# A mixture-of-experts block on one core: late items get a slot order of their own, result rows begin in DRAM, and small items split their second activation part first

## What is computed

```
logits = h @ w_router + b_router
top_val, top_idx = lax.top_k(logits, 4)            # 4 of 32 experts for each token
gates = jax.nn.softmax(top_val)
hgu = lax.ragged_dot(h[tok], w_gate_up, group_sizes) + b_gate_up[e_sorted]   # [2048 rows] x [1024, 2048] per expert
act = min(glu, 7) * sigmoid(1.702 * min(glu, 7)) * (clip(lin, -7, 7) + 1)
out = (lax.ragged_dot(act, w_down, group_sizes) + b_down[e_sorted]) * gates  # x [1024, 1024] per expert
moe = segment_sum(out, tok)
h = layernorm(alpha * h + moe)
```

## Time and profile before

| | us |
|---|---|
| median of 3 runs | 1948.08 |
| lowest and highest | 1943.51, 1948.17 |
| the profiled execution | 1949.36 |
| its span, first to last instruction | 1947.7 |
| busy: PE, DVE, ACT, POOL | 1837.7, 1667.0, 1351.6, 508.4 |
| mean granted clock | 0.978 |

### The profile page before, as it was taken

The page is one execution under the profiler, slowest core; times in us unless marked ns, Lnnn a source line. Parts: engine busy times, 40 slices in busy tenths (PEclk is TensorE's granted clock), DMA queues, the critical chain, the costliest instruction groups (busy, mean ns, idle before and its releaser), DMA issues.

```text
span 1947.7 us, 28549 instructions
## 1 busy us (share of the span) xinstructions
PE 1837.7 (94%) x8415; PEld 1438.3 (74%) x8415; DVE 1667.0 (86%) x1783; ACT 1351.6 (69%) x1777; POOL 508.4 (26%) x395
## 2 busy tenths in 40 slices
PE   6999999998989998999999999999899999999887
PEld 3657767787768876877777777777777777777665
DVE  6899987348775477989999999999899999999877
ACT  4556865214346525788889888888888888898775
POOL 6671000000000105523422423423133322323121
PEclk7999999999999997999999999999899999999988
DMA  8222225332110156999999999999999999999995
GB/s 318 86 108 86 87 67 203 121 102 73 54 44 23 38 179 213 340 401 386 392 395 395 388 396 391 386 387 395 331 396 401 391 388 383 398 390 345 345 322 201
DMA packets 133073, 523.37 MB, mean 269 GB/s; under 512 B 15145, under 2 KB 20425, under 8 KB 112848
## 3 DMA queue, kind: packets, MB, share of 16 engines
q1 hardware_dynamic: 118704, 492.45, 66.5%
q0 software_dynamic: 14304, 30.11, 5.6%
HBM read 512.76 MB, written 19.29 MB: 273 GB/s over the span
## 4 chain that ended last, share of the span: by engine, by line
PE 63%; DVE 12%; DMA 10%; ACT 8%; issue 5%; SPq 1%; ACTq 0%; DVEq 0%; POOL 0%
PE ps L1150 28%; DMA arena<-in_w_gate_up 8%; PE ps L1386 5%; PE ps L1434 5%; PE ps L1199 3%; DVE split L2852 3%; PE ps L1377 3%; ACT arena_r L2047 2%; PE ps L1415 2%; PE ps L1391 2%; PE ps L1613 2%; PE ps L1482 2%; PE ps L1066 2%; ACT split L2047 2%; ACT arena L2076 1%
## 5 line engine op out<-in xcount | busy, mean ns | idle before, releaser
L1150 PE MATMUL ps<-split,xTs 128*128 128x512 f32 x2016 | 505.3, 399 | 11.3 <-DVE split L2852 7.7
L1150 PEld LDWEIGHTS ps<-split,xTs 128*128 128x128 f32 x2016 | 379.5, 191 | 106.5 <-DVE split L2852 21.0
L2852 DVE TENSOR_TENSOR split<-arena,split 128x2048 fp32r<-128x2048 f32 x166 | 377.1, 2286 | 16.6 <-ACT split L2047 14.9
L2047 ACT ACTIVATE split<-arena 128x1024 fp32r<-128x1024 f32 x332 | 330.9, 1052 | 32.0 <-DMA arena<-in_w_gate_up 25.4
L2852 DVE TENSOR_TENSOR split<-ring,split 128x2048 fp32r<-128x2048 f32 x106 | 242.8, 2305 | 0.4 <-ACT split L2047 0.4
L856 POOL DMA_INDIRECT y_rows<-arena,slots x33 | 146.2, 4431 | 345.2 <-issue 291.5
L2047 ACT ACTIVATE split<-ring 128x1024 fp32r<-128x1024 f32 x212 | 212.7, 1057 | 7.0 <-DMA ring<-in_w_gate_up 2.9
L2852 DVE TENSOR_TENSOR arena_r<-arena,arena_r 128x2048 fp32r<-128x2048 f32 x83 | 189.7, 2285 | 3.4 <-ACT arena_r L2047 3.4
L1150 PE MATMUL ps<-arena_r,xTs 128*128 128x512 f32 x672 | 182.6, 406 | 6.7 <-ACT arena_r L2047 4.9
L1150 PE MATMUL ps<-split,aTs 128*128 128x512 f32 x672 | 168.3, 396 | 15.9 <-DVE aTs L2911 15.9
L2047 ACT ACTIVATE arena_r<-arena 128x1024 fp32r<-128x1024 f32 x166 | 171.7, 1055 | 14.5 <-DMA arena<-in_w_gate_up 13.8
(11 more groups left out here) (484 smaller groups left out, 3127.0 us busy)
## 6 DMA issues: line engine op xcount, KB each, us to landing
arena<-in_w_gate_up SPq DMA_DIRECT2D x170, 1024.0 KB, 14.2
ring<-in_w_gate_up SPq DMA_DIRECT2D x102, 1024.0 KB, 14.7
arena<-in_w_down SPq DMA_DIRECT2D x79, 1024.0 KB, 14.3
ring<-in_w_down SPq DMA_DIRECT2D x57, 1024.0 KB, 14.6
ring<-in_w_in SPq DMA_DIRECT2D x23, 1024.0 KB, 5.0
ring<-in_w_out SPq DMA_DIRECT2D x8, 1024.0 KB, 5.2
ring<-in_mod_w SPq DMA_DIRECT2D x10, 512.0 KB, 9.1
ring<-in_mod_w SPq DMA_DIRECT2D x4, 1024.0 KB, 5.0
```

The source lines that it names most:

```text
L1150: m = mm(ps[:, banks + q, :], lhs[:, x_, k, :], w[:, q * 512:(q + 1) * 512], start=start, stop=stop)
L2047: A(split_part(0, c), chunk(it, c), ACT.Copy).then_inc(sig("hi_ready"), 1)
L2852: V.tensor_tensor(split_pair(1, p), slot_tile(it.slot(p)), split_pair(0, p), ALU.subtract).then_inc(sig("lo_ready"), 1)
```

## The change

There are three edits.

1. `y_dram` is begun out of `h1_dram` and not out of `h1` in SBUF, and ACT doesn't wait for `y_begun`. POOL's wait stays.
2. A late item's tiles go to the slots of `LATE_SLOTS`. For each tile `before_in` finds which tile, of the item itself or of the one before, used the slot last, and SP waits for that one. Since the one program text of the loop serves the first late item (behind a small one with the old order) and the others, the later of the two tiles is waited for. `late_item`'s counts of loads per slot follow.
3. In small items, the loop's and the late ones, ACT does `act_high(1)` ahead of `split_high(22, 23)` and DVE `act_low(1)` ahead of `split_low(10)`.

```diff
--- before.py
+++ after.py
@@ -111,17 +111,31 @@
 class Item:
 
 
-    def __init__(self, i, small, next_small, pairs, at, rows, loads, begin=0, joined=None):
+    def __init__(self, i, small, next_small, pairs, at, rows, loads, begin=0, joined=None, late=False):
         self.i, self.small, self.next_small = i, small, next_small
+        self.late = late
         self.pairs, self.at, self.rows, self.joined = pairs, at, rows, joined
         self.loads, self.begin = loads, begin
 
     def slot(self, j):
-        return (j + self.begin) % SLOTS
+        return LATE_SLOTS[j] if self.late else (j + self.begin) % SLOTS
+
+    def before_in(self, j, before):
+
+        own = [q for q in range(j) if self.slot(q) == self.slot(j)]
+        if own:
+            return self, own[-1]
+        last = before.last_in(self.slot(j))
+        if before.late:
+            last = max(last, max(q for q in range(EXPERT_TILES) if q % SLOTS == self.slot(j)))
+        return before, last
 
     def last_in(self, s):
         return max(j for j in range(EXPERT_TILES) if self.slot(j) == s)
 
+LATE_SLOTS = (6, 7, 4, 5, 0, 1, 6, 7, 4, 5, 2, 3)
+
+
 def uses(s):
     return 2 if s < EXPERT_TILES - SLOTS else 1
 
@@ -144,7 +158,7 @@
 def late_item(j, back=0):
 
     return Item(j + (BEFORE_LATE - back), True, True, j * PAIRS + (BEFORE_LATE - back) * PAIRS,
-                j + (BEFORE_LATE - back - BIG), j * 32 + ((BEFORE_LATE - back) * 32 - BIG * 16), lambda s: j * (16 * uses(s)) + 48 * (LOOPS + 1), 0, j + (BEFORE_LATE - back - BIG))
+                j + (BEFORE_LATE - back - BIG), j * 32 + ((BEFORE_LATE - back) * 32 - BIG * 16), lambda s: j * (16 * LATE_SLOTS.count(s)) + (48 * (LOOPS + 1) + 16 * (uses(s) - LATE_SLOTS.count(s))), 0, j + (BEFORE_LATE - back - BIG), True)
 
 
 
@@ -692,10 +706,7 @@
                 expert_tile(first_item(), j, 0)
             def slot_free(it, before, j):
 
-                if j < SLOTS:
-                    it, j = before, before.last_in(it.slot(j))
-                else:
-                    j = j - SLOTS
+                it, j = it.before_in(j, before)
                 wait_alone(sp, sig("lo_ready"), sp.to_reg(it.pairs + (LEAD + j + 1)))
 
             def item_tiles(it, before):
@@ -826,7 +837,7 @@
             pool.wait_ge(sig("idx0_ready"), 1)
             gather(idx_first[:, 0:1])
             for t in range(TC):
-                pool.dma_start(y_dram[t * P:(t + 1) * P, :], h1[:, t, :]).then_inc(sig("y_begun"), 16)
+                pool.dma_start(y_dram[t * P:(t + 1) * P, :], h1_dram[t * P:(t + 1) * P, :]).then_inc(sig("y_begun"), 16)
 
             pool.wait_ge(sig("oh_ready"), 1)
             by_k = lambda x: x.rearrange("p (t k) e -> p t k e", t=TC)
@@ -2051,7 +2062,6 @@
                 act.wait_ge(sig("xt_ps"), q + 1)
                 high(xTs, q, 7 - 6 * q, sig("xt_hi"), P)
             act.wait_ge(sig("h1_stored"), 16 * TC)
-            act.wait_ge(sig("y_begun"), 16 * TC)
 
             def run(it):
 
@@ -2126,8 +2136,8 @@
                     split_high(20, 22)
                     sigmoid(1)
                     next_high(0)
+                    act_high(1)
                     split_high(22, 23)
-                    act_high(1)
                     next_high(1)
                     split_high(23, 24)
                     return
@@ -2936,8 +2946,8 @@
                     act_low(0)
                     split_low(9)
                     activation(1)
+                    act_low(1)
                     split_low(10)
-                    act_low(1)
                     next_low(0)
                     split_low(11)
                     next_low(1)
```

## The result

Six runs of the changed kernel gave a median of 1929.27 us (1926.83 to 1932.83), beside 1941.41 us (1934.92 to 1948.17) for six of the kernel before. The ratio is 0.9936 with a 95% interval from 0.9915 to 0.9957: 12.4 us faster, clear of the 0.3%. The time lies in the range given, 3.3 us above the forecast. The gain is a little over half of the 22.4 us summed. That the time still came so near is in part luck: the kernel before is 6.7 us lower in the median of six runs than in that of the first three. From 1948.08 us the same ratio would have led to some 1936, still in the range but 10 us above the forecast. The profiled execution has a span of 1928.8 us (before: 1947.7), so the spans alone, at 18.9 us, would flatter the change.

What follows compares the result with a forecast made beforehand. PE, DVE and DMA were taken as nearly full in the steady stretch, with room in late items and the expert phase's start. Terms 6.8 + 17.6 - 2 = 22.4 us off 1949.4 gave 1927.0; forecast 1926, range 1917 to 1939.

Steps and rivals of the forecast that it cites:

- a gain of 17.6 us: Late items: the new slots keep loads streaming, so three items take 98.0 us on PE instead of 115.6.
- the rival of starved late items: Late items: six slots in a burst don't carry the stream; gain 9.6 instead of 17.6 us, time 1934, chance 0.12.
- The price by bytes: Late items: 12.79 MB each at the steady stretch's 388 GB/s, giving 33.0 us.
- I take 6.8, since PE is the engine without a gap after it: Expert phase start: PE's 4.9 us gap goes and 1.9 us of low clock come back.
- from about 760.5: Expert phase start: POOL can issue item 1's gather behind its store at 759.48, from about 760.5 us.
- A slower copy up to some 28 us is covered: Expert phase start: item 0's matmuls hide a DRAM to DRAM copy of up to some 28 us.
- Start hidden: Expert phase start: first items' loads or the gather set the pace, edit 1 gives nothing; 1932.5 us, chance 0.08.
- they don't absorb the gain: Expert phase start: DMA engines wait for slots, at 0.33 and 13 GB/s behind PE's gap, so the gain stays.
- sum +2 us: Small items: the new order costs 2 us in all, most of DVE's stall being absorbed by the loads.
- The full price of 18 x 0.55 = 9.9 us: Small items: upper bound of the new order's cost, 9.9 us over 18 items.
- 0.1 us each, 1.5 us: Steady stretch: full DMA engines absorb part of the stall, leaving 0.1 us in each of 15 small items, 1.5 us.
- DMA keeps the first two: Late items: DMA sets the first two, so the new order costs 0.5 us only in the last.

Runs made afterwards that it cites:

- no_order_again: The changed kernel without its third edit, run once more beside the changed kernel on one chip: 1923.48 us, ratio 0.9895 to the kernel before.
- early gather: Edits 1 and 2 without 3, with POOL issuing item 1's gather behind the third store of slot rows, not the eighth: 1924.48 us, ratio 0.9902 to before.
- only_slots: Edit 2 alone, the late items' slot order, on the kernel before: 1927.26 us against 1947.46, ratio 0.9909.
- only_order: Edit 3 alone, both engines' new order in small items, on the kernel before: 1954.93 us against 1947.46, ratio 1.0047.
- only_act_order: Only ACT's half of edit 3, on the kernel before: 1945.20 us against 1942.78, ratio 1.0008.
- only_dve_order: Only DVE's half of edit 3, on the kernel before: 1955.01 us against 1945.49, ratio 1.0065.
- no_order: The changed kernel with its third edit taken back: 1929.70 us, ratio 0.9913 to the kernel before.
- source_wait_kept: The kernel before with only the source of the result-row copies changed to DRAM, ACT's wait kept: 1940.08 us, ratio 0.9985.

## Why the prediction came out as it did

The range held and the sign was right, and so was the order of size of the largest term. Two of the three terms of the sum were mis-sized, both to the bad side.

**Edit 2, "a gain of 17.6 us": right in size and in the wait that it removes; the pace of the items behind it was met partly by luck.** Alone it measured 17.7, with an interval from 14.2 to 21.0, so the agreement to a tenth says nothing. The late items were to take 33.0, 33.0 and 32 us and took 32.7, 33.0 and 33.0 (98.7 against 98.0). The second keeps the stream full, 393 GB/s against the 388 taken, and the rival of starved late items (36 each) is out. But the stream doesn't set the 33.0: the last item takes it as well, with DMA at 0.80 and 303 GB/s, and the three kernels with edit 2 but no edit 3 and the old gather take 32.4 to 32.9, the second in `no_order_again` 32.45 at 408 GB/s. In these items DVE is the fullest engine, 31.56 of 32.97 us in the last. The price by bytes and the real pace happened to agree.

The Trainium skill's page HBM Reference, section Specifications, gives some 358 GB/s as a core's effective share, and more for a core that streams alone. The row of this case, 393 GB/s over such an item, agrees with the second and is above the first.

**Edit 1, "I take 6.8, since PE is the engine without a gap after it": the step that failed.** It measured 1.0 us alone, with an interval from a gain of 3.1 to a loss of 1.2. PE's gap and the low clock behind it did go (the window right behind the old gap, 755.88 to 760.67, has a granted clock of 1.00). But PE had a gap after it, which I priced away in the paragraph on POOL: "from about 760.5" assumed that POOL's stores keep the 0.97 us of the earlier trace rows. That row stands in a stretch where DVE is idle, as its next subtract waited 10.6 us for ACT. With the gap gone, DVE's subtracts run there, the stores beside them take up to 3.06 us each, and the gather leaves at 768.5. "A slower copy up to some 28 us is covered" looked at the copy, which was fast, and not at what runs beside it. The rival "Start hidden", which had a chance of 0.08, is what came for this term. The gather isn't all of it. PE waited 5.94, 1.21 and 3.55 us for it in the three profiles of the changed kernel, and longest of all, 6.86, in `no_order_again`, which has the lowest median of all kernels here. The early gather then showed that a second limit lies just behind: item 1's weights, in a stretch where the DMA engines are full at 157 to 180 GB/s. My argument that they don't absorb the gain read the gap's 13 GB/s and not the 20 us behind it. What fills them is shown only so far: not the layernorm's rows, and not the time of the stores' own packets (1.1%), but slow packets of the weights. Whether these are slow because of the stores beside them isn't shown, as the 16 stores were not taken out; every later item reads them.

There was also less to win than one profile said. PE's gap was 4.89 us in the profiled execution of before; in the profiles of the four single-edit kernels that keep ACT's wait and the old source (`only_slots`, `only_order`, `only_act_order`, `only_dve_order`) it is 1.89, 3.03, 2.29 and 1.77, in the mean of the five 2.8. So about 2 of the 6.8 us stood in that one execution only. The same holds for a longer stretch. From DVE's first `idx_first` to ACT's output of the third big item the profiled execution of before took 162.2 us, at the long end: the same four took 161.2, 161.5, 157.5 and 159.4. The mean of these five is 160.4. The eight profiles with edit 1 whole lie between 153.6 and 159.2, mean 157.2. So some 3 us are gained up to that point on average, of which the medians of whole executions show 1.0 with an interval that just reaches 3.1. Whether the rest is given back later or lies in the spread of single profiles stays open.

**Edit 3, "sum +2 us": the mechanism was right and the absorbed share was mis-sized.** The steps were: DVE stands still for 0.5 us, PE's 0.88 us go, and 0.5 and 0.9 us come in their place. Measured: 0.48; PE's wait on `act_low` gone; 0.48 and 0.39 in the last small item before the late ones, 0.47 and 0.67 at 1670 us. The full price of 18 x 0.55 = 9.9 us, which I kept as the upper bound, is nearly what it costs alone (9.1); beside the others it is 4.9. The step that failed is "0.1 us each, 1.5 us": I took the DMA share of 1.01 as proof that the loads set the pace of the loop and would swallow half a microsecond. They set it only in some pairs. Where they don't, before takes 66.6 us and the change 67.1. The late items didn't absorb it either, though I took "DMA keeps the first two": without edit 3 the second and third take 32.4 to 32.5 us each in `only_slots`, `no_order` and `no_order_again`, with it 33.0 in all three profiles of the changed one. Why the stall costs 4.9 us beside the slot order and 9.1 alone stays open; the interval of the single run reaches from 6.0 to 12.1, so the two may be nearer than they look.

The three terms as measured, -1.0, -17.7 and +4.9, make -13.8 (against -22.4 summed); the change measured -12.4, -12.0 and -14.8 in three sets. The best version here is the change without its third edit, ratios 0.9913 and 0.9895; the early gather adds nothing to it that these runs can show.

## What to carry to other kernels

Where a ring of buffers changes its phase between two kinds of item, count the distance from each load to the buffer's last use: four tiles starved this stream of 1 MB loads, six kept it going. When a wait is removed, durations read inside the old gap are those of an idle machine (here POOL's stores with DVE standing still); take them from a busy stretch, and ask what the freed work will now run beside. Look at a gap in several profiles before it is priced: this one was 4.89 us in one and 1.8 to 3.0 in four others. And a busy share of 1 for DMA doesn't prove that compute has slack: look at how long the shortest rounds take, since a stall added to the fullest engine shows in those.

## What was not expected of the hardware

The slowest of the four copies from DRAM to DRAM landed sooner than the slowest of the same rows out of SBUF: 4.4 to 8.4 us per 512 KB against 3.7 to 17.8. And POOL's issue of an indirect store of 128 slot rows, 0.97 to 1.16 us when no subtract of DVE runs beside it and at any DMA share up to 1.01, takes up to 6.52 us (`source_wait_kept`) when subtracts do: it ends 0.84 to 0.91 us after the end of one. The small direct load that POOL issues between these stores takes 0.61 to 0.62 us with a subtract beside it and without. One long round stands at the same place in all 14 profiles of this case, whatever the edit: the pair of items that ends near 1440 us takes 69.1 to 73.0 us instead of about 67, and between 1360 and 1370 us, ahead of it, the DMA engines are full at only 115 to 261 GB/s (before 198, after 181). No run looked into it.
